# First head's softmax and the first picks ahead of tile 1's steps on all engines; the buffer with the modulation rows joins the gathers at the twelfth pick

## What is computed

```python
# peer_ffn, for each chunk of 128 tokens (two chunks: "tile 0" and "tile 1")
q = einsum('cd,de->ce', xc, w_q).reshape(C, 8, 2, 128)        # 8 heads, 2 halves
s = einsum('chpk,pnk->chpn', q, sub_keys)                     # 128 scores a half
sv, si = top_k(s, 16)
cand = sv[:, :, 0, :, None] + sv[:, :, 1, None, :]            # 256 candidates
top_v, top_pos = top_k(cand.reshape(C, 8, 256), 16)
eid = take_along_axis(cand_id, top_pos)                       # 16 experts a head
gate = softmax(top_v)
act = gelu(einsum('cd,chkd->chk', xc, expert_u[eid]))
y = einsum('chk,chkd->cd', gate * act, expert_v[eid])         # 128 picks a token
...
x = x + g2 * y
return rmsnorm(x, final_g)
```

## Time and profile before

| what | us |
|---|---|
| median of 3 executions | 1461.84 |
| lowest and highest of them | 1461.76, 1462.53 |
| the profiled execution's own time | 1459.33 |
| span from its first to its last instruction | 1457.5 |

### The profile page before, as it was taken

The page is one execution under the profiler, slowest core; times in us unless marked ns, Lnnn a source line. Parts: engine busy times, 40 slices in busy tenths (PEclk is TensorE's granted clock), DMA queues, the critical chain, the costliest instruction groups (busy, mean ns, idle before and its releaser), DMA issues.

```text
span 1457.5 us, 14866 instructions
## 1 busy us (share of the span) xinstructions
PE 1314.0 (90%) x4972; PEld 830.8 (57%) x4972; DVE 812.7 (56%) x1682; ACT 416.2 (29%) x1038; POOL 643.6 (44%) x643
## 2 busy tenths in 40 slices
PE   9999999999999999999998979977877787776786
PEld 8888687747888687747757645533333333332332
DVE  2465367441466367433137775889887654544455
ACT  3332243211332243212222332322313232122123
POOL 0546667430446677431302344364544454444440
PEclk9999999999999999999999999998988999999989
DMA  8453335255453335256165999999999999999995
GB/s 346 165 182 136 139 125 208 98 220 202 151 196 123 145 121 219 90 228 256 35 255 229 373 420 410 420 419 420 420 420 420 420 419 421 420 420 420 420 421 209
DMA packets 53446, 406.68 MB, mean 279 GB/s; under 512 B 6117, under 2 KB 8698, under 8 KB 10746
## 3 DMA queue, kind: packets, MB, share of 16 engines
q0 software_dynamic: 36864, 268.45, 44.6%
q1 hardware_dynamic: 15418, 136.23, 23.9%
q10 hardware_dynamic: 1088, 1.05, 0.4%
HBM read 403.58 MB, written 1.07 MB: 278 GB/s over the span
## 4 chain that ended last, share of the span: by engine, by line
PE 63%; DMA 24%; DVE 7%; issue 3%; ACT 3%; POOL 1%; ACTq 0%; POOLq 0%; DVEq 0%
PE pj L664 23%; PE bank L1093 10%; PE pj L708 9%; DMA ring<-in_peer_uv,vM 9%; PE pj L679 7%; DMA yT<-in_peer_uv,vM 5%; PE bank L812 3%; DMA hv<-in_peer_uv,vM 3%; DMA more_rows<-in_peer_uv,vM 3%; DMA qM<-in_peer_uv,vM 3%; PE pj L963 2%; PE bank L638 1%; PE bank L913 1%; DVE tri L1855 1%; DMA qvE<-in_peer_uv,vM 1%
## 5 line engine op out<-in xcount | busy, mean ns | idle before, releaser
L664 PE MATMUL pj<-xT,ring 128*128 128x256 f32 (+2 forms) x1536 | 324.4, 371 | 1.8 <-ACTq L1146 1.7
L664 PEld LDWEIGHTS pj<-xT,ring 128*128 128x128 f32 (+1 forms) x1536 | 277.5, 188 | 42.8 <-issue 3.1
L592 POOL TENSOR_SCALAR more_rows<-more_rows,lbt 128x256 f32<-128x256 f32 x168 | 176.7, 1052 | 16.4
L626 POOL DMA_INDIRECT ring<-in_peer_uv,vM x101 | 120.9, 1197 | 120.3 <-PE bank L1093 109.3
L590 POOL TENSOR_SCALAR mod_part<-more_rows,lbt 128x256 f32<-128x256 f32 x24 | 25.9, 1080 | 275.2 <-issue 120.8
L708 PE MATMUL pj<-ring,yT 128*128 128x512 f32 x320 | 140.3, 594 | 0.0
L593 POOL TENSOR_TENSOR mod_part<-mod_part,more_rows 128x256 f32<-128x256 f32 x168 | 128.0, 762 | 14.0
L1316 ACT ACTIVATE rope<-vM 128x4 f32<-128x4 f32 (+3 forms) x84 | 17.1, 204 | 406.9 <-DVE big L1855 324.7
L1093 PE MATMUL bank<-ring,causal 128*128 128x512 f32 x200 | 99.9, 638 | 19.8 <-ACT causal L1324 19.8
L1093 PE MATMUL bank<-ring,tri 128*128 128x512 f32 x204 | 96.4, 611 | 16.3 <-ACT tri L1324 16.3
L708 PEld LDWEIGHTS pj<-ring,yT 128*128 128x128 f32 x320 | 59.9, 190 | 71.1 <-issue 71.1
(11 more groups left out here) (370 smaller groups left out, 2160.2 us busy)
## 6 DMA issues: line engine op xcount, KB each, us to landing
ring<-in_units SPq DMA_DIRECT2D x44, 2048.0 KB, 9.3
more_rows<-in_w_ada SPq DMA_DIRECT2D x24, 1024.0 KB, 4.8
ring<-in_units SPq DMA_DIRECT2D x2, 1536.0 KB, 6.9
ring<-in_units SPq DMA_DIRECT2D x2, 1024.0 KB, 8.1
ring<-in_peer_uv,vM POOLq DMA_INDIRECT x101
big<-in_mem SPq DMA_DIRECT2D x1, 1024.0 KB, 5.1
x<-in_x SPq DMA_DIRECT2D x1, 1024.0 KB, 11.3
kM<-cT ACTq DMA_DIRECT2D x4, 256.0 KB, 3.5
```

The costliest lines, as they stand in the source:

```text
L592: do(g.tensor_scalar(mod_w[:, c, :], mod_w[:, c, :], silu_c[:, c:c + 1], None, ALU.mult))
L626: pool.indirect_dma_start(row_slot[k], None, d["peer_uv_2"], bass.IndirectOffsetOnAxis(ap=expert[:, t, j:j + 1], axis=0))\
L664: ins = nc.tensor.matmul(pj[s][0:n, 2 * m + first:2 * m + stop], ring[:, slot, at:at + n], act[:, c, first:stop], start=(c == 0), stop=(c ...
```

## The change

Four lists of the order and the slot table are changed, nothing of the arithmetic. On TensorE `Zu` goes ahead of `K1at`, and the first picks are taken in between the query products instead of behind them. On VectorE `H2t` and `GT1` go ahead of `OMu`, the first dot ahead of `NMu`, the second ahead of `Zu`; `H2u` stays behind the third dot; `XP2` comes behind dot 9 instead of 8. On ScalarE the first diagonals go ahead of `Zu` and of the copies `K1bt`. On GpSimd slot 6 (`hv`) is first used for pick 12 instead of pick 6, so that picks 6 to 11 go into slots 0 to 5 again.

```diff
@@ PE_ORDER, last block
-            Y5 O1u Zt O0v K0at E0t O0w K0bt E1t K1at Zu K1bt E2t K0au W4 K0bu E3t W5 W7 EU0 K1au W11 K1bu W15 EU1 W21
-            K20 W27 K21 W31 K22 W32 K23 W36 E4 W37 E5 W40 K30 W42 K31 W45 K32 W49 K33 W55 E6 E7 W256"""]
+            Y5 O1u Zt O0v K0at E0t O0w K0bt E1t Zu K1at W1 K1bt W2 E2t W3 K0au W5 K0bu E3t W8 EU0 K1au W12 K1bu W16
+            EU1 W21 K20 W27 K21 W31 K22 W32 K23 W36 E4 W37 E5 W40 K30 W42 K31 W45 K32 W49 K33 W55 E6 E7 W256"""]
@@ ACT_LAST
-ACT_LAST = """Xu BU BK BQa BQb SK S0 S1 MT S2 BV P0 P1 S3 S4 P2 S5 P3 P4 P5 OMt Zt K0at E0t T1 K0bt E1t OMu Zu K1bt W1
-    E2t W5 E3t W7 K0bu W8 T2 W11 EU0 W18 K1bu W20 T3 W21 EU1 W35 K23 W38 E4 W39 E5 W51 T4 W57 K33 W61 E6 W62
+ACT_LAST = """Xu BU BK BQa BQb SK S0 S1 MT S2 BV P0 P1 S3 S4 P2 S5 P3 P4 P5 OMt Zt K0at E0t T1 K0bt E1t OMu W1 Zu W2
+    K1bt W3 E2t W6 E3t W8 K0bu W10 T2 W13 EU0 W18 K1bu W20 T3 W21 EU1 W35 K23 W38 E4 W39 E5 W51 T4 W57 K33
@@ DVE_LAST
-DVE_LAST = """Xu S0 S1 S2 PL0 PL1 N0 N1 S3 N2 S4 S5 N3 N4 Y1 N5 OMt Y5 NMt Zt Rt0 XP1 OMu H2t NMu D1 Zu D3 H2u D4 GT1
-    D5 Rt1 D8 XP2 D9 Rt2 D15 Rt3 D16 GT2 D18 XP3 D37 GT3 D44 Rt4 D50 Rt5 D54 XP4 D62 GT4 D63 Rt6 Rt7 D72 XP5
+DVE_LAST = """Xu S0 S1 S2 PL0 PL1 N0 N1 S3 N2 S4 S5 N3 N4 Y1 N5 OMt Y5 NMt Zt Rt0 XP1 H2t GT1 OMu D1 NMu D2 Zu D3 H2u
+    D5 Rt1 D9 XP2 D11 Rt2 D15 Rt3 D16 GT2 D18 XP3 D37 GT3 D44 Rt4 D50 Rt5 D54 XP4 D62 GT4 D63 Rt6 Rt7 D72 XP5
@@
-NEW_SLOTS = {0: ("", range(0, 7)), 18: ("K1", (7, 8)), 41: ("K2", (9, 10)), 67: ("K3", (11, 12, 13)), 74: ("E7", (14,))}
+NEW_SLOTS = {0: ("", range(0, 6)), 12: ("H2u", (6,)), 18: ("K1", (7, 8)), 41: ("K2", (9, 10)), 67: ("K3", (11, 12, 13)), 74: ("E7", (14,))}
```

More of the change, by code:

```diff
@@ L72 @@
     Le18 HO2 HN2 HO3 HN3 LN"""
-ACT_LAST = """Xu BU BK BQa BQb SK S0 S1 MT S2 BV P0 P1 S3 S4 P2 S5 P3 P4 P5 OMt Zt K0at E0t T1 K0bt E1t OMu Zu K1bt W1
-    E2t W5 E3t W7 K0bu W8 T2 W11 EU0 W18 K1bu W20 T3 W21 EU1 W35 K23 W38 E4 W39 E5 W51 T4 W57 K33 W61 E6 W62
-    E7 W65 T5 W96 T6 W129 T7 W148 FN0 W256 FN1"""
+ACT_LAST = """Xu BU BK BQa BQb SK S0 S1 MT S2 BV P0 P1 S3 S4 P2 S5 P3 P4 P5 OMt Zt K0at E0t T1 K0bt E1t OMu W1 Zu W2
+    K1bt W3 E2t W6 E3t W8 K0bu W10 T2 W13 EU0 W18 K1bu W20 T3 W21 EU1 W35 K23 W38 E4 W39 E5 W51 T4 W57 K33
+    W61 E6 W62 E7 W65 T5 W96 T6 W129 T7 W148 FN0 W256 FN1"""
 DVE_ORDER = """F0 N FP0 R0 R1 R2 R3 Da01 KR Da02 S0 Db01 P0 Db02 L01 Da03 S1 L02 AD Db03 Da04 F1 AD S2 Da05 L03 Da06
```

## The result

The changed kernel takes 1465.72 us in the median of 20 runs, and the kernel before 1460.74 us, also in 20 runs. The ratio is 1.0034, with a 95% interval of 1.0026 to 1.0042: **slower by 5.0 us** (3.8 to 6.1). The forecast was 1464.8 us, 3.0 us above before, with a range of 1461.5 to 1467.5. The profiled execution took 1463.54 us with a span of 1461.7 us, which is 4.2 us above both numbers of the profile of before (1459.33 and 1457.5). It is the third fastest of the 20 executions.

A forecast was written before the change was run, and what follows sets the result against it. The prediction took DMA bytes as the bound behind 840 us and idle DMA time ahead of 818 us as all an edit changes. Dry time of 6.2 against 2.6 us gave +3.0 on 1461.84: 1464.8 us, range 1461.5 to 1467.5.

The forecast's parts named there:

- TensorE's new wait: `K1at` queued behind `Zu` leaves TensorE idle from 784.7 to 792.6 us, 7.2 us more idle than before.
- the sum: DMA queue up to pick 9: dry for 6.2 us against 2.6, costing +1.9 to +3.6 us, taken as +3.0.
- with `K1at` ready: On TensorE from 784.7 to 792.6 us: `K1at` could run but stands behind the waiting `Zu`.
- the first issue "does not move": On GpSimd: the first gather's issue at 783.65 waits for `XP1`, which has the same instructions ahead; no loss at 785 to 801.
- From pick 10 on gathers are ready in time: Gathers behind pick 9: no further dry time; `K1bu` ends at about 839.4, 3 us inside pick 18's limit.
- the forecast's case: The whole kernel ends +1.9 to +4.4 us against before; 60 in 100.
- the clearly slower rival: TensorE: `Zu` starts at 793.4 and two low clock stretches occur instead of one; +5.8 us, 1467.6; 13 in 100.
- `hv`'s move to pick 12 costs nothing of its own: Slot table on GpSimd: no cost, since `H2u` is done by about 800 and pick 12 issues behind 820.
- Behind 840 us the end is set by bytes: From 840 to 1436 us, DMA share 1.01 at 419 GB/s: no engine's earlier work makes a gather end sooner.
- 4.3 us as the most that an order can win: Missing DMA work from 801 to 818 us, 3.5 plus 0.8 us, bounds any reordering behind the first gather.
- the faster rival: Dry spots ahead of 818 us close because buffers come free sooner; 1459.6, or 1457.5 with all of it; 7 in 100.
- The "same" rival: From 840 to 1436 us, late DMA work only eats slack; 1461.8, or +1 at most; 20 in 100.

The follow-up runs named there:

- e6: The changed kernel with `OMu` ahead of `H2t` and `GT1` on VectorE again; ratio to the kernel before 1.0042.
- e1: The changed kernel with `K1at` ahead of `Zu` on TensorE again, six slots kept; 1461.63 us, ratio to the kernel before 1.0009.
- e7: The kernel before once more with nothing changed, one run for its trace; span 1457.0 us.
- e3: The changed kernel with the old slot table (seven slots, `hv` at pick 6), all orders as changed; ratio to the kernel before 1.0033.
- e2: The kernel before with only the changed slot table (`hv` joins at pick 12); ratio to the kernel before 1.0014.
- e10: The changed kernel with `OMu` ahead of `H2t` and `GT1`, `K1at` ahead of `Zu`, and the old seven slots; ratio to the kernel before 1.0009.
- e4: The changed kernel with `K1at` ahead of `Zu` on TensorE and the old seven slots; ratio to the kernel before 1.0018.
- e12: The kernel of e4 once more with nothing changed, one run for its trace; span 1457.6 us.
- e5: The kernel before with only `Zu` put ahead of `K1at` on TensorE, seven slots; ratio to the kernel before 1.0035.

## Why the prediction was right, and where it was not

**TensorE's new wait: right.** `Zu` started at 793.16 for 792.6, pick 0's product at 799.61 for 799.0, and the issues of picks 6 to 9 were at 801.76, 807.05, 809.22 and 814.51 for 801.2, 806.5, 808.7 and 814.0. All are 0.5 to 0.6 us late, and that amount is there from `Zu` on. The first issue took 1.77 us for 1.17, beside `H2t` (e6, without `H2t` there, has 1.17 again). The prediction had this at up to 0.8 us and left it out of the sum. Its reason for it was misread: `hv`'s issue of 1.80 us starts at 799.63, and `H2u` had ended at 799.36, so what ran beside it was a dot. The row that does show it is the third issue of the kernel before, 1.72 us instead of 0.94 beside the same `H2t`:

```profile
786.37 1.72 POOL L626 DMA_INDIRECT qvE<-in_peer_uv,vM  x1 [0.30 <-issue]
```

In the changed kernel the third issue takes 0.94 us: the cost moved from the third issue to the first.

The granted clock fell as supposed: `Zu` and `K1at` together took 1.76 + 4.69 = 6.45 us from start to start for 4.45, which is the 2.0 us taken. The case of two such stretches did not occur (1.00 from 798 us on). The rule of the Trainium skill that the prediction named (SBUF — State Buffer, section "SBUF: two separate sides") speaks of descriptors that can't be written while VectorE holds the shared port pair; the longer issue agrees with it, at 0.6 us. For instructions with two inputs in SBUF the same section limits the lock to a GpSimd instruction that reads SBUF, and no run here shows which case this is. One statement was wrong: "with `K1at` ready". Its bank was being read by `OMu` until 788.8 in this order, as e1 shows. The sum is not touched by this, since it counts from `Zu`'s start.

**The sum: sign and mechanism right, size low.** On the profile's scale the +3.0 was +4.2. It is made up of three parts, by the missing work counted above:

- 801 to 818 us: 2.2 us more. This is the dry queue that the prediction computed. Over the whole stretch that it named, 801 to 821 us, the rate is 274 GB/s for 335 before, which is 6.95 - 4.05 = 2.9 us more. So the term of +3.0 was right in its own place.
- 785 to 801: 0.9 us more. This is the term that the prediction had wrong: it set this stretch at nothing, since the first issue "does not move". Its start was 0.3 us later and it took 0.6 longer.
- 818 to 840: 1.1 us more, of which 0.7 lies ahead of 821 us and is counted above. "From pick 10 on gathers are ready in time" was wrong. Pick 8's issue was 0.5 us late and took 1.88 us instead of 0.94, and it landed at 816.2 for 814.4, and `K1bu` ended at 842.5 for 839.4. Between them TensorE had a further wait of 2.02 us at 835.23, for the diagonal of pick 10, which ScalarE makes together with the one of pick 11, and that pick's dot starts only at 831.54. The bound that I gave for pick 18's issue was 842.5, and it was issued at 842.77.

A second trace of the kernel before (e7) misses 3.5 us from 801 to 821 where the first misses 4.05, so each of these parts is good to about half a microsecond.

In the timed runs the loss is 5.0 us (3.8 to 6.1), above the profile's 4.2 and above the upper end of the forecast's case (4.4), but below the clearly slower rival (5.8). Against the forecast of 1464.8 the 1465.72 looks better than it is, and that is luck: the three executions that the forecast started from had their median at 1461.84, 1.1 us above the 1460.74 of the 20. In the difference, +5.0 for +3.0, the forecast is 2.0 us off. The rival decides from a `Zu` start behind 793. It was 793.16, so one of its two parts, the longer first issue, was there, and the other, the second low stretch, was not.

**"`hv`'s move to pick 12 costs nothing of its own": right here, wrong as a general statement.** In the changed kernel the old slots bring nothing (e3). In the kernel before they are worth 2.0 us (e2), since there pick 6 waits 4.6 us longer for pick 0 than it did for `H2u`. In e3's trace the old slot does bring 2.4 us up to pick 18, and they are gone by pick 41.

**"Behind 840 us the end is set by bytes", and 4.3 us as the most that an order can win: wrong in what it leaves out.** The DMA share of 1.01 is a mean over 596 us. The gathers also wait for TensorE, at pick 18 and at pick 41, and from 870 to 900 us a wait for ScalarE and the low clock behind it take back what was won. That did not touch this forecast, because a loss carries through to the end (+4.1 us at pick 41, +4.2 in the span). It does touch the faster rival: e10 wins 3.1 us of the 4.3 and keeps 1.1 of them in its span, and none in its time. The "same" rival needed slack to eat in this stretch. In these traces a lead was lost there and a lag was not made up.

## What to carry to other kernels

Before a task that waits is put ahead of one that seems ready, look up what the second one waits for too, and count the whole row behind both: here one swap of two tasks on TensorE costs as much as the whole change, and the earlier first picks never earn it back. Missing rate in one stretch is only an upper bound for a gain, and the gain lasts only until the gathers wait for another engine again: here an earlier TensorE waited longer for ScalarE and could lose 1.7 us more to the low clock. A loss on the path has no such limit. Compare two traces from an event that both share (here the first gather's issue), since single executions of one kernel can differ ahead of it by as much as the effect that is being sought, and look where the traced execution stands among the timed ones.

## What the runs showed of the hardware

- An issue of an indirect gather on GpSimd took 1.77 us beside `H2t`'s two 1024-wide instructions (a multiply and an add, both operands in SBUF) (783.48 to 785.97) and 1.17 us beside `OMu`'s 512-wide ones. It happened in every kernel with `H2t` at that place (changed, e1, e3, e4, e12), and not in those without. In the nine profiles in which `H2t` lies on the third issue, it is that one that takes 1.71 to 1.73 us, and it takes 0.94 in the other five.
- Behind the same wait of 2.9 us at 675 us, a place ahead of everything in which the kernels differ, TensorE's eight transposes ran in 1.09 to 1.10 us in seven traces and in 1.97 in the other seven; the kernel before has both. Whether a wait costs clock can't be read from its length alone: a single execution is a sample of it.
- Behind waits of 5.6 to 8.5 us, in the changed kernel, e3, e5 and e6, the eight transposes took 1.97 us each time.
- At 872 us two products took 3.54 us from start to start behind a wait of 2.85 us in one execution (e4), and 5.22 behind a wait of 2.83 in another of the same kernel (e12): 1.7 us.
